# A hybrid decoder step on one core: mLSTM sample states as one fp32r product, HGRN sample values turned after the scores, and a reordered start

## The reference

```python
def trunk(x, c, ...):
    mod = silu(c) @ ada_w + ada_b                      # 2048 -> 6 * 2048, adaLN
    sh1, sc1, g1, sh2, sc2, g2 = split(mod, 6)
    h = rms_norm(x) * (1 + sc1) + sh1
    x = x + g1 * token_mixer(h, ...)                   # w_in: 2048 -> 18448
    h = rms_norm(x) * (1 + sc2) + sh2
    x = x + g2 * conv_ffn(h, ...)                      # w_up, gelu, w_down; FF = 5632
    return rms_norm(x, final_norm_w)
# mLSTM, per head (8 heads, keys of 128, values of 256), chunk-wise:
C = decL * C + einsum('bhs,bhsd,bhsv->bhdv', wk, kc, vc)
n = decL * n + einsum('bhs,bhsd->bhd', wk, kc)
# HGRN2, per head (16 heads, 128 x 128):
S = exp(bL) * S + einsum('bhsk,bhsv->bhkv', kc * exp(bL - b), vc)
```

## Time and profile before

| | |
|---|---|
| median of 3 runs | 2273.9 us (2272.72 to 2274.05) |
| the profiled execution | 2273.14 us, span of its instructions 2271.4 us |
| mean granted TensorE clock | 0.991 |
| busy: TensorE, its weight loads | 2215.2 us (98%), 2079.6 us (92%) |
| busy: VectorE, ScalarE, GpSimd | 1113.8, 989.0, 335.9 us |
| DMA | 460.03 MB, mean 203 GB/s |

### The profile page before, as it was taken

One profiled execution on the slowest core, in us unless ns is written; L12 is line 12 of the kernel. 1 busy time (PEld: TensorE's weight loads), 2 busy tenths in 40 slices (PEclk: granted clock), 3 DMA queues, 4 the chain that ended last, 5 costly groups with the idle time before them and its releaser, 6 DMA issues. The chain is left out here.

```text
span 2271.4 us, 42271 instructions
## 1 busy us (share of the span) xinstructions
PE 2215.2 (98%) x17370; PEld 2079.6 (92%) x17370; DVE 1113.8 (49%) x1506; ACT 989.0 (44%) x1367; POOL 335.9 (15%) x522
## 2 busy tenths in 40 slices
PE   6999999999999999999999997999999999999998
PEld 3589999999999999999999996999999999999997
DVE  3246455464564444443444555555555555544443
ACT  3336553564464335453544435434344434433333
POOL 2000212321222222121111232000000000110000
PEclk8999999999999999999999999999999999999999
DMA  9986666657666666766665779555555555555553
GB/s 350 362 275 195 214 190 203 198 187 218 202 199 187 213 200 194 245 206 218 221 218 186 227 246 313 159 168 164 167 163 167 160 167 166 176 162 169 173 167 107
DMA packets 407411, 460.03 MB, mean 203 GB/s; under 512 B 14843, under 2 KB 379955, under 8 KB 406433
## 3 DMA queue, kind: packets, MB, share of 16 engines
q1 hardware_dynamic: 394192, 410.64, 56.6%
q0 software_dynamic: 12240, 46.03, 6.4%
q10 hardware_dynamic: 833, 1.26, 0.2%
HBM read 431.48 MB, written 26.39 MB: 202 GB/s over the span
## 5 line engine op out<-in xcount | busy, mean ns | idle before, releaser
L753 PE MATMUL ps<-xh,whi 128*128 128x288 f32 x3968 | 1195.2, 301 | 18.3 <-DVE xl L1711 8.5
L1654 DVE TENSOR_TENSOR wlo<-raw,whi 128x1024 fp32r<-128x1024 f32 x584 | 735.8, 1261 | 942.2 <-ACT whi L1227 933.2
L755 PE MATMUL ps<-xh,wlo 128*128 128x288 f32 x3968 | 1172.8, 296 | 0.0
L754 PE MATMUL ps<-xl,whi 128*128 128x288 f32 x3968 | 1171.8, 295 | 0.0
L1227 ACT ACTIVATE whi<-raw 128x1024 fp32r<-128x1024 f32 x584 | 616.9, 1058 | 794.2 <-PE ps L755 778.0
L753 PEld LDWEIGHTS ps<-xh,whi 128*128 128x128 f32 x3968 | 747.8, 188 | 69.3 <-issue 52.0
L754 PEld LDWEIGHTS ps<-xl,whi 128*128 128x128 f32 x3968 | 747.3, 188 | 0.0
L755 PEld LDWEIGHTS ps<-xh,wlo 128*128 128x128 f32 x3968 | 747.2, 188 | 0.0
L753 PE MATMUL ps<-ffh,whi 128*128 128x288 f32 x704 | 209.2, 297 | 0.0
L755 PE MATMUL ps<-ffh,wlo 128*128 128x288 f32 x704 | 208.4, 296 | 0.0
L754 PE MATMUL ps<-ffl,whi 128*128 128x288 f32 x704 | 208.3, 296 | 0.0
(11 more groups left out here) (408 smaller groups left out, 1597.8 us busy)
## 6 DMA issues: line engine op xcount, KB each, us to landing
raw<-in_w_in SPq DMA_DIRECT2D x288, 512.0 KB, 4.3
raw<-in_w_up SPq DMA_DIRECT2D x176, 512.0 KB, 3.5
raw<-in_w_down SPq DMA_DIRECT2D x88, 512.0 KB, 3.5
araw<-in_ada_w SPq DMA_DIRECT2D x74, 512.0 KB, 5.6
uraw_x<-in_ada_w SPq DMA_DIRECT2D x36, 512.0 KB, 8.6
raw<-in_w_out SPq DMA_DIRECT2D x32, 512.0 KB, 3.5
top<-in_ada_w SPq DMA_DIRECT2D x24, 512.0 KB, 7.9
afill<-in_ada_w SPq DMA_DIRECT2D x18, 512.0 KB, 7.8
```

The costliest lines, as they stand in the source:

```text
L753: mm(o, whi[:, s, kk, cols], hi[:, kt0 + kk, :], start=first and kk == 0, stop=False)
L754: mm(o, whi[:, s, kk, cols], lo[:, kt0 + kk, :], start=False, stop=False)
L755: x = mm(o, wlo[:, s, kk, cols], hi[:, kt0 + kk, :], start=False, stop=last and kk == KC - 1)
L1654: TT(wlo[:, s], raw[:, s], whi[:, s].bitcast(F32), ALU.subtract).then_inc(lo_done, 1)
```

## The change

Four things.

1. The sample states of mLSTM are formed as HGRN's are. Keys are weighted on VectorE before they are turned (`kw`, from a broadcast row of weights that L1030 now carries as 32 further columns), rounded to fp32r, copied, and the rest put beside them in the free columns, so that one product of 32 rows sums high x high, high x low and low x high. GpSimd does the same with the values, once a group. The key tile of the samples is turned in `vT`, and `c1`, `c2` and the normalisers read fp32r.
2. In HGRN's `tr` the third value tile is turned after the scores, and only that one waits for GpSimd's last cast.
3. At the start VectorE normalises group 0 first and the other three after the second chunk's low part; from unit 3 on SyncE is two chunks less ahead; TensorE makes 40 transposes of the identity, which nobody reads, before the first piece.
4. Six GpSimd instructions for masks become one, and an unread semaphore goes.

```diff
+WARM = 40
...
-    return RING if u == BESIDE else min(EARLY_LOADS, 2 * RING + pieces_ahead(u - 1, c // 2) // 4)
+    return RING if u == BESIDE else min(EARLY_LOADS, 2 * RING + pieces_ahead(u - 1, c // 2) // 4 - 2)
...
-        bmask = sb("bmask", [P, 4, 2], stack=mixer)
-        rmask = sb("rmask", [P, 2], stack=mixer)
+        bmask = sb("bmask", [P, 4, 2], F32R, stack=mixer)
...
-        mK = sb("mK", [P, 3, P], stack=ml_mem)
+        mK = sb("mK", [P, 2, P], stack=ml_mem)
+        mKs = sb("mKs", [P, P], F32R, stack=ml_mem)
+        kw = sb("kw", [P, TS], stack=ml_mem)
...
-        mVM = sb("mVM", [P, 2, MV], stack=ml_mem)
+        mVM = sb("mVM", [P, 2, MV], F32R, stack=ml_mem)
...
                 if u == BESIDE:
+                    pe.wait_ge(small_c, 3)
+                    for _ in range(WARM):
+                        tr(R[:, 2, P:2 * P], ident[:, :])
                     for _ in range(EARLY_FIRST):
                         next(started)
...
                 if o == "tr":
-                    pe.wait_ge(hg["vc"], 4 * (i + 1))
+                    pe.wait_ge(hg["vc"], 4 * i + 1)
                     pe.wait_ge(hg["snew"], n + FREE)
-                    for t in range(3):
-                        x = tr(R[:, 1, P * t:P * (t + 1)], v[:, P * t:P * (t + 1)])
-                    x.then_inc(hg["vt"], 1)
+                    for t in range(2):
+                        tr(R[:, 1, P * t:P * (t + 1)], v[:, P * t:P * (t + 1)])
                     yield
                     pe.wait_ge(hg["cp"], 2 * (i + 1))
...
+                    pe.wait_ge(hg["vc"], 4 * (i + 1))
+                    tr(R[:, 1, TP:TPAD], v[:, TP:TPAD]).then_inc(hg["vt"], 1)
+                    yield
...
-                    mm(R[:, 0, 0:EM], ones8[:, :], mLR[:, :], start=True, stop=True).then_inc(ml["bc"], 1)
+                    mm(R[:, 0, 0:EM + TS], ones8[:, :], mLR[:, :], start=True, stop=True).then_inc(ml["bc"], 1)
                     yield
                     pe.wait_ge(ml["cp"], 2 * (i + 1))
-                    for t in range(3):
+                    for t in range(2):
                         x = tr(R[:, 1, P * t:P * (t + 1)], k[:, P * t:P * (t + 1)])
...
                 if o == "vT":
-                    pe.wait_ge(ml["vc"], i + 1)
-                    pe.wait_ge(ml["mk"], 3 * (n + 1))
+                    pe.wait_ge(ml["vc"], 4 * (i + 1))
+                    pe.wait_ge(ml["mk"], 2 * (n + 1))
                     pe.wait_ge(ml["arg"], 3 * (n + 1))
                     pe.wait_ge(ml["es"], n + 1)
+                    pe.wait_ge(ml["ks"], 4 * (n + 1))
+                    tr(R[:, 1, MV:MV + P], k[:, TP:TPAD])
...
-                        x = mm(R[:, g, :], mK[r, 2, :], mVM[r, :, :].rearrange("p a b -> p (a b)"), start=True, stop=True)
+                        x = mm(R[:, g, :], mKs[r, :], mVM[r, :, :].rearrange("p a b -> p (a b)"), start=True, stop=True)
...
-                    for t in range(3):
+                    for t in range(2):
                         A(mK[:, t, :], R[:, 1, P * t:P * (t + 1)], ACT.Copy, scale=wkcol[:, t, bass.ds(h, 1)]).then_inc(ml["mk"], 1)
...
                     A(mV[:, 0:2, 0:MV], R[:, 0, :].rearrange("p (a b) -> p a b", a=2), ACT.Copy).then_inc(ml["mv"], 1)
+                    A(mKs[:, :], R[:, 1, MV:MV + P], ACT.Copy)
...
-            for g in range(4):
-                normalise(1, xT, merged, g)
+            normalise(1, xT, merged, 0)
             unit(1)
             samples(1, merged, 0, 0, KT)
             lo(N_HG, 0, True)
             low_parts(1, merged, 0)
-            for k in range(1, RING):
+            lo(N_HG, 1, True)
+            for g in range(1, 4):
+                normalise(1, xT, merged, g)
+            for k in range(2, RING):
                 lo(N_HG, k, True)
...
                     TT(tok8(arg[:, TPAD:4 * P]), by8(R[:, 0, TP:T]), tok8(amask_s[:, :]), ALU.add).then_inc(ml["arg"], 1)
+                    s = mWQ[:, 2 + j, TP:TPAD]
+                    TT(by8(kw[:, :]), third8(s, 0), by8(R[:, 0, EM:EM + TS]), ALU.mult).then_inc(ml["ks"], 1)
+                    dve.wait_ge(ml["qk"], n + 1)
+                    dve.wait_ge(ml["ks"], 4 * n + 1)
+                    nc.vector.tensor_copy(third8(s, 1).bitcast(F32R), by8(kw[:, :])).then_inc(ml["ks"], 1)
+                    dve.wait_ge(ml["ks"], 4 * n + 2)
+                    nc.vector.tensor_copy(third8(s, 3), third8(s, 1)).then_inc(ml["ks"], 1)
+                    TT(third8(s, 2), by8(kw[:, :]), third8(s, 1), ALU.subtract).then_inc(ml["ks"], 1)
...
                 nc.gpsimd.tensor_copy(mWQ[:, 4:8, :], mSQ[:, 4:8, :]).then_inc(ml["vc"], 1)
+                v = mWQ[:, 4:8, TP:TPAD].rearrange("p h (j e) -> p h j e", e=32)
+                pool.wait_ge(ml["vc"], 4 * i + 1)
+                nc.gpsimd.tensor_copy(v[:, :, :, 8:16].bitcast(F32R), v[:, :, :, 0:8]).then_inc(ml["vc"], 1)
+                pool.wait_ge(ml["vc"], 4 * i + 2)
+                nc.gpsimd.tensor_copy(v[:, :, :, 16:24], v[:, :, :, 8:16]).then_inc(ml["vc"], 1)
+                G(v[:, :, :, 24:32], v[:, :, :, 0:8], v[:, :, :, 8:16], ALU.subtract).then_inc(ml["vc"], 1)
...
-                    G(mVM[:, :, :], mid(mV[:, 2, 0:MV], 2), rep_last(rmask[:, :], MV), ALU.mult).then_inc(ml["vm"], 1)
+                    G(mVM[:, :, :], mid(mV[:, 2, 0:MV], 2), rep_last(smask[:, :], MV), ALU.mult).then_inc(ml["vm"], 1)
```

More of the change, by code:

```diff
@@ L45 @@
 ROW_T = ROW_WK
-CONST_ALL = 46
+CONST_ALL = 41
 CONST_CS = 1
@@ L375, in build @@
         mWG = sb("mWG", [P, 4, T], stack=ml_mem)
-        mLR = sb("mLR", [MH, EM], stack=ml_mem)
+        mLR = sb("mLR", [MH, EM + TS], stack=ml_mem)
         es = sb("es", [P, TS + NS], stack=ml_mem)
@@ L450, in build @@
                                           "scaled", "y", "yt", "snew", "out", "st")}
-        ml = {n: sem("ml_" + n) for n in ("pad", "zero", "cp", "vc", "sig", "gate", "lr", "bc", "kT", "qk", "mk", "es", "arg",
+        ml = {n: sem("ml_" + n) for n in ("pad", "zero", "cp", "vc", "sig", "gate", "lr", "bc", "kT", "qk", "ks", "mk", "es", "arg",
                                           "dx", "pm", "qi", "vT", "mv", "vm", "c0", "n0", "num", "dn", "ss", "f", "rs", "cs", "y",
@@ L456, in build @@
         x1_m, x1_p, x1_a, x1_sq, x1_acc = (sem(n) for n in ("x1_m", "x1_p", "x1_a", "x1_sq", "x1_acc"))
-        ab_ready, ab_lead, ab_tail = sem("ab_ready"), sem("ab_lead"), sem("ab_tail")
+        ab_lead, ab_tail = sem("ab_lead"), sem("ab_tail")
         ff_conv, ff_gelu, ff_y, ff_hi, ff_lo = (sem(n) for n in ("ff_conv", "ff_gelu", "ff_y", "ff_hi", "ff_lo"))
@@ L1083, in ml_step @@
                         yield
-                    mm(R[:, 2, MV + NS:MV + 2 * NS], mK[:, 2, :], bmask[:, :, :].rearrange("p a b -> p (a b)"), start=True, stop=True).then_inc(ml["stp"], 1)
+                    mm(R[:, 2, MV + NS:MV + 2 * NS], mKs[:, :], bmask[:, :, :].rearrange("p a b -> p (a b)"), start=True, stop=True).then_inc(ml["stp"], 1)
                     yield
@@ L1097, in ml_step @@
                         r = slice(32 * g, 32 * g + 32)
-                        x = mm(R[:, g - 2, :], mK[r, 2, :], mVM[r, :, :].rearrange("p a b -> p (a b)"), start=True, stop=True)
+                        x = mm(R[:, g - 2, :], mKs[r, :], mVM[r, :, :].rearrange("p a b -> p (a b)"), start=True, stop=True)
                     x.then_inc(ml["st2"], 1)
@@ L1467, in evict @@
                     if u == 2 and not first:
-                        act.wait_ge(ml["vc"], i + 1)
+                        act.wait_ge(ml["vc"], 4 * (i + 1))
                     if u == 4 and first:
@@ L1587, in each @@
                         act.wait_ge(ab_tail, 2 * i + FREE)
-                        A(abuf[:, :, 2:2 + TP], ps[:, 0, :, 0:TP], ACT.Copy).then_inc(ab_ready, 1)
+                        A(abuf[:, :, 2:2 + TP], ps[:, 0, :, 0:TP], ACT.Copy)
                         A(seq3(abuf[:, :, 2 + TP:AB], 2 + LS)[:, :, :, 2:2 + LS], seq3(ps[:, 0, :, TP:T], LS), ACT.Copy).then_inc(bank_free[0], 1)
@@ L1835, in gate_rows @@
                     dve.wait_ge(row_a, 7)
+                    nc.vector.tensor_copy(LR[:, EM:EM + TS], r[:, 13, TP:T])
                     nc.vector.memset(rowpad, 0.0).then_inc(row_p, 1)
@@ L1892, in rows_of @@
             def rows_of(h):
-                TSC(mLR[:, :], LR[:, 0:EM], ident[0:MH, bass.ds(h, 1)], None, ALU.mult).then_inc(ml["lr"], 1)
+                TSC(mLR[:, :], LR[:, 0:EM + TS], ident[0:MH, bass.ds(h, 1)], None, ALU.mult).then_inc(ml["lr"], 1)
             def ml_step(j, o, n, i):
@@ L1991, in first_part @@
                         dve.wait_ge(ml["cp"], 2 * 4)
-                        dve.wait_ge(ml["vc"], 4)
+                        dve.wait_ge(ml["vc"], 16)
                         dve.wait_ge(ml["gate"], 4)
@@ L2153, in _ @@
             cst_(nc.gpsimd.tensor_scalar(amask_s[:, :], maskf_s[:, :], -NEG, NEG, ALU.mult, ALU.add))
-            cst_(nc.gpsimd.memset(bmask[:, :, :], 1.0))
```

(6 more changed lines are left out.)

## The result

The changed kernel takes **2259.19 us** (median of 4 runs, 2255.23 to 2259.42), the kernel before beside it 2273.98 (2272.72 to 2274.18). The ratio is 0.9932, with a 95% interval of 0.9919 to 0.9944: faster by 0.7%, 14.8 us. The forecast was 2260.1. The profiled execution of the changed kernel took 2259.29 us with a span of 2257.5, against 2273.14 and 2271.4 before. The sum came out within 1 us, but that is in part luck: mLSTM gave 1.9 us more than its terms, and 1.6 us that no term had were given back later. The marks show where.

The account below looks back on a forecast made before the run. TensorE, issuing back to back, was taken to bound the kernel from about 72 us on, the order of transfers before. Terms summed to -13.8: 2273.1 - 13.8 + 0.8 = 2260.1 us, range 2255 to 2266.5.

Parts of the forecast that it names:

- The state products: mLSTM's 16 pairs of sample products, L1091 and L1098: fp32r drops one of two passes, -8.5 us.
- the length of the pass: One fp32r pass of 512 columns in mLSTM's state products: 0.82 ns a column, 0.53 us with the gap between passes.
- The bound that I had set aside: State products at the main matmuls' 0.46 ns a column: a pair takes 0.35 instead of 1.06 us, -11.4 us.
- The full-rate rival: mLSTM's fp32r state products run at the main matmuls' rate: -11.4 us for that term, 2257.2 us in all; chance 0.13.
- a pass under 0.4 us: Sign of a wrong prediction: L1091's pass in mLSTM's state products under 0.4 us (or over 0.9).
- The normaliser: mLSTM's 8-column normaliser product loses one of two records: at most 0.1 us in each of 8 heads, booked at 0.1.
- The broadcast: mLSTM's L1030 grows from 328 to 360 columns, in two passes, over 8 heads: +0.4 us.
- The split: Four more VectorE instructions per head in mLSTM's step arg: hidden in six heads, +0.9 us from the last two.
- a new wait over 1 us: Sign of a wrong prediction: a new TensorE wait longer than 1 us between 72 and 1340 us.
- HGRN: First head in three of four groups: two transposes and the scores no longer wait for GpSimd's casts, -2.6 us.
- The start: Before 72 us: with two weight chunks fewer ahead and a fuller DMA queue unit 3 starts earlier, -3.9 us.
- The empty queue: DMA share sags between 57 and 67 us: 1.2 us of empty queue, ended by issuing unit 3's tiles from about 54.

Follow-up runs that it names:

- run 8: The changed kernel with the 8-column normaliser product L1093 read as float32 again; 2258.01 us.
- run 9: The changed kernel with each pair of mLSTM state products issued twice over; 2262.34 us.
- run 10: The changed kernel with HGRN's step as before: three value transposes after the whole chain of casts, then the scores; 2261.13 us.
- run 3: The changed kernel with all four groups normalised before unit 1's modulation, as before; 2259.21 us.
- run 4: The changed kernel without the 40 transposes at the start; 2257.93 us.
- run 2: The changed kernel with the old number of weight chunks ahead of the units; 2262.57 us.
- run 1: The kernel before with the mLSTM part alone and the fewer mask constants; HGRN's step, the start and the loads as they were; 2264.98 us.
- run 7: The changed kernel with the values turned first in step vT, after the first of four key operations, and the key tile last; 2256.26 us.
- run 5: The changed kernel with four weight chunks fewer ahead from unit 3 on, in place of two; 2277.49 us.
- run 6: The changed kernel with three weight chunks fewer ahead, in place of two; 2257.94 us.
- run 11: The changed kernel with three chunks fewer ahead and the keys' transpose behind the values' in step vT; 2256.80 us.
- run 12: The changed kernel with four chunks fewer ahead, ScalarE making a unit's high parts only behind its copy of that unit's rows; 2274.42 us.

## Why the prediction was right, and where it wasn't

**The state products** were forecast at -8.5 and gave -10.07 (20.82 us for the 16 pairs from main matmul to main matmul before, 10.74 after). The step that failed is the length of the pass. I had inferred 0.82 ns a column from the durations of two records with different types, L1013's 256 fp32r columns and L967's 128 float32 columns, as if both streamed alike. They don't. For float32 the 0.82 was about right: L1091's passes of 257 columns start 0.218 us apart (889.50 in run 8's fences), the scores' of 128 columns 0.111, so 0.83 ns a column; and the broadcast's 32 columns more move its second pass from 0.380 to 0.406 us behind its first, 0.81 ns a column. The fp32r pass costs 0.235 us for 512 columns (run 9), 0.46 ns a column. (The 0.53 us from one float32 pass of a pair to the next is not all columns: two fp32r passes start 0.34 us apart in run 9, 0.10 more than one of them adds, and by that estimate the float32 pass is 0.43 us of columns.) The bound that I had set aside, the main matmuls' 0.46 ns, was the right rate, and a fixed part of 0.43 - 0.24 = 0.19 us behind the pass, where I had 0.11, kept the gain below that bound's 11.4. The full-rate rival was right in its mechanism, and 1.3 us too high in its price. The trace of the kernel before could not have decided it by L1013's duration, but its distance to the next main matmul, 0.31 us for 256 columns against the 0.43 now measured for 512, points at 0.46 too. So one sign that I had named for a wrong prediction, a pass under 0.4 us, did appear. The Trainium skill, "TensorE: Matmul & The Clock Gate", section "Back-to-back issue gap", gives 216 ns as the gap of an isolated matmul of 512 columns. Run 9 agrees with it within 0.02 us, so it was wrong to let L1013 decide against that rule.

**The normaliser** was booked at -0.1, with 0.8 as its upper limit, and gave -0.9 (14.72 us in eight blocks before, 13.83 after; run 8 puts it back). **The broadcast**: the stretches of the step qk went from 2.150 to 2.095 us while a transpose of 0.107 left them, so +0.05 each, +0.4 in all, as forecast.

**The split** was forecast at +0.9. The two late heads gave +1.1 (waits of 2.1 us against 1.0), the six others only the moved transpose. The first and the last of the four instructions in VectorE's timeline:

```profile
1241.50 0.17 DVE L1920 TENSOR_TENSOR kw<-mWQ,R 128x32 f32<-128x32 f32 x1
...
1242.08 0.18 DVE L1926 TENSOR_TENSOR mWQ<-kw,mWQ 128x32 f32<-128x32 f32 x1
```

They take 0.17 to 0.18 each and the chain 0.76 from the first's start to the last's end, near the 0.8 of the working. Another sign that I had named for a wrong prediction, a new wait over 1 us, did appear by its letter: 1.31 us, of which 0.48 are old. These terms add up to -9.5, where the stretch from chunk 196 to 318 gave -9.16 against my -7.3. Of the difference 0.05 is the first head's step qk, which lies ahead of chunk 196, and 0.14 the distances between main matmuls in the stretch; the rest is spread.

**HGRN** was forecast at -2.6, and gave -2.83 in the change and 2.73 when undone (run 10). The waits inside the other heads cost nothing.

**The start** was forecast at -3.9, and gave -3.6. Most of its argument held. No gain of the early normalise (run 3) or the transposes (run 4) shows, and without the new load order the gain falls to 0.74 at chunk 40 (run 2), no more than the 0.65 of run 1 with the old start. The empty queue did fill: the DMA share of 0.98 and 0.80 is 1.09 from 57 to 64 and 1.06 from 64 to 67 in the changed kernel. But SyncE issued unit 3 at 57.23, where the working had it from about 54 on. Unit 3 was forecast for 68 and came at 68.32. The last tile of unit 7 was forecast for near 137.7 and used at 138.1, so the slack was enough. I had said the DMA would allow up to 5.5 us. Three fewer gave marks 1.1 to 1.6 earlier, and the fourth met a bound which that count of slack didn't contain: the order of work on ScalarE and VectorE.

**What was missing** is the 1.56 us given back behind the mixer, which no term had. The lines of that stretch, in the changed kernel and in run 7 (TensorE; between them a stretch of the first kernel with the columns us, PE busy, PEclk, DMA share, GB/s):

```profile
1366.99 3.45 PE L1154 MATMUL R<-mixo,ones 128*128 128x288 f32 x8 [2.50 <-ACT mixo L1584]
1370.37 2.32 PE L781 MATMUL R<-afill,cs 128*32 128x256 f32 x32
```

```profile
1366.00:1370.00 4.00, 3.01 (x8) 0.72 1.10 349
```

```profile
1365.46 2.21 PE L1154 MATMUL R<-mixo,ones 128*128 128x288 f32 x8 [2.50 <-ACT mixo L1584]
1367.60 1.93 PE L781 MATMUL R<-afill,cs 128*32 128x256 f32 x32
```

The same work behind the same wait of 2.5 us takes 3.45 + 2.32 us in one and 2.21 + 1.93 in the other, 1.6 us more, where the granted clock has fallen to its 1.2 GHz level for part of it. The profiles of the change and of runs 1, 3, 4, 5, 6, 9, 10 and 11 show this fall; those of the kernel before and of runs 2, 7, 8 and 12 do not. What decides whether it comes isn't settled. TensorE did the same ahead of it in both, and no run here controls it. It is also a likely cause of a part of the spread of each kernel's runs. The mean granted clocks fit, and prove nothing: the changed kernel's run of 2255.23 us has 0.996, its other three, of 2259.1 to 2259.4, have 0.990 to 0.993, and in runs 3, 6, 8, 9 and 10 the fastest run is the one at 0.996 as well, though not in runs 7 and 11.

So the sum was right to 0.1 us against the span (-13.8 and -13.86) because 1.9 too little for mLSTM and 0.2 too little for HGRN stand against 0.3 too much for the start, 1.56 given back, and 0.18 in the tail. That these errors cancel is luck. (The lower end of the range, 2255, is 0.7 below its own terms: 2257.2 - 1.5 = 2255.7.)

## What to carry to other kernels

When TensorE issues back to back, price a change of type by the distance between the instructions around it, and take the rate of a pass from rows of the same type; a duration of one record holds a fixed part, and two such parts of different types can't be subtracted. Where an order of loads bounds the start, try the order one step at a time: 2 chunks fewer ahead gained about 3 us, 3 fewer perhaps 1 more, and 4 fewer lost 18 us, because two engines had other work queued behind the late chunk. An agreement of the total proves no term; marks at the same places of the program in both traces do.

## What the runs showed of the hardware

- A float32 pass costs about 0.83 ns a column (passes of 257 and 128 columns, 0.218 and 0.111 us apart), an fp32r pass 0.46 (run 9), and float32 makes two of them. A pair of 32-row products of 512 columns, measured to the next main matmul, goes from 1.06 to 0.43 us, of which about 0.19 is fixed.
- TensorE's clock rises while it does transposes alone. In the changed kernel's own profile it is at 2.4 GHz before they begin, so other profiles have to show it. In run 7 the clock is at its 1.2 GHz level when the 40 transposes begin, and back at 2.4 before they end; without them (run 4) it stays low until the first pieces have run to about 50. The timeline of run 7, its stretches, and those of run 4 (us, then busy time of PE, PEld, DVE, ACT, POOL, then PEclk, DMA share, GB/s):

```profile
40.03 6.11 PE L734 MATMUL R<-ident 128*128 128x128 f32 x40
```

```profile
40.00:42.00 2.00, 2.00 (x11) 2.00 (x12) 1.65 (x4) 1.55 (x4) 0.05 (x1) 0.50 1.08 366
42.00:44.00 2.00, 2.00 (x14) 2.00 (x13) 0.52 (x2) 1.97 (x4) 0.00 (x0) 0.69 1.05 405
44.00:46.00 2.00, 2.00 (x21) 2.00 (x20) 2.00 (x2) 2.00 (x3) 0.00 (x0) 1.00 1.03 429
```

```profile
44.00:46.00 2.00, 0.00 (x0) 0.00 (x0) 1.29 (x2) 2.00 (x3) 0.00 (x0) 0.50 1.06 441
...
48.00:50.00 2.00, 2.00 (x10) 2.00 (x10) 2.00 (x3) 0.00 (x0) 0.00 (x0) 0.50 0.98 410
50.00:52.00 2.00, 2.00 (x16) 2.00 (x15) 2.00 (x2) 0.00 (x0) 0.20 (x1) 0.94 1.02 398
```

The Trainium skill, "TensorE: Matmul & The Clock Gate", "Part 4: PE-mode transpose", says that transposes don't count as TensorE being busy for the clock. These rows say otherwise for float32 transposes of 128x128, and run 11's profile does too (0.51, 0.63, 1.00 in the same three stretches). No gain in time shows, since unit 3's transfer absorbs what the faster pieces gain.
